# Twelve weight loads per layer of a two-block transformer kernel, each split into a transfer of 120 and one of 8 partitions

## The reference

```python
def peer_ffn(x, w_q, sub_keys, u_tab, v_tab):
    ...
        q = (xc @ w_q).reshape(c, PEER_HEADS, 2, PEER_HALF)
        sc = jnp.einsum('chpd,hpnd->chpn', q, sub_keys).astype(jnp.float32)
        top_s, top_i = lax.top_k(sc, PEER_TOPK)
        ...
        gate = jax.nn.softmax(best_s, axis=-1).astype(xc.dtype)
        u = u_tab[idx]
        act = jax.nn.gelu(jnp.einsum('chkd,cd->chk', u, xc), approximate=False)
        vsel = v_tab[idx]
        return jnp.einsum('chk,chkd->cd', gate * act, vsel)
```

## Time and profile before

| | us |
|---|---|
| time, median of 3 runs | 2322.83 |
| lowest and highest run | 2317.26, 2323.83 |
| profiled execution, its span | 2321.1 |
| DVE busy | 1526.8 (66%) |
| PE busy | 1973.8 (85%) |
| DMA queue of the rows (q0), share of 16 engines | 55.9% |
| DMA queue of SP's loads (q1), share of 16 engines | 20.5% |

### The profile page before, as it was taken

One profiled execution on the slowest core, in us unless ns is written; L12 is line 12 of the kernel. 1 busy time (PEld: TensorE's weight loads), 2 busy tenths in 40 slices (PEclk: granted clock), 3 DMA queues, 4 the chain that ended last, 5 costly groups with the idle time before them and its releaser, 6 DMA issues.

```text
span 2321.1 us, 26066 instructions
## 1 busy us (share of the span) xinstructions
PE 1973.8 (85%) x8576; PEld 1298.3 (56%) x8576; DVE 1526.8 (66%) x3664; ACT 671.8 (29%) x1257; POOL 1232.9 (53%) x824
## 2 busy tenths in 40 slices
PE   7999999999999889887778777798799877777776
PEld 6889998789988764443223222387644433323222
DVE  6441115531117878887888877677798878888776
ACT  6644336644436522111011100156221110111000
POOL 6748867658873256555444444132465554444441
PEclk9999999999999889999999999998899999999999
DMA  5435544435555279999999999662799999999996
GB/s 178 146 112 196 182 162 158 156 117 191 182 178 191 100 296 420 421 420 421 421 421 421 421 420 422 258 221 85 274 410 421 421 421 421 421 422 421 421 421 278
DMA packets 118012, 700.21 MB, mean 302 GB/s; under 512 B 13968, under 2 KB 13968, under 8 KB 51856
## 3 DMA queue, kind: packets, MB, share of 16 engines
q0 software_dynamic: 73728, 536.90, 55.9%
q1 hardware_dynamic: 44176, 161.96, 20.5%
HBM read 697.76 MB, written 1.05 MB: 301 GB/s over the span
## 4 chain that ended last, share of the span: by engine, by line
PE 39%; DMA 39%; DVE 14%; POOL 3%; issue 3%; ACT 2%; DVEq 0%; SPq 0%; POOLq 0%; ACTq 0%
PE ps L637 38%; DMA late_row<-in_table,arena 21%; DMA arena<-in_table,arena 17%; DVE arena L2345 2%; POOL w_split L1222 2%; DVE diag L2355 1%; DVE late_row L2345 1%; DVE arena L2035 1%; DMA row_sb<-in_table,arena 1%; DVE w_split L2021 1%; DVE arena L2319 0%; ACT w_split L1348 0%; POOL arena L1308 0%; PE ps L669 0%; ACT hT_hi L1371 0%
## 5 line engine op out<-in xcount | busy, mean ns | idle before, releaser
L1222 POOL TENSOR_TENSOR w_split<-raw,w_split 128x1024 fp32r<-128x1024 f32 x256 | 623.4, 2459 | 340.4 <-ACT w_split L1348 337.5
L637 PE MATMUL ps<-late_row,diag 128*128 128x512 f32 x1000 | 480.1, 624 | 124.6 <-DVE diag L2355 124.6
L637 PE MATMUL ps<-hT_hi,w_split 128*128 128x256 f32 (+1 forms) x2688 | 521.5, 292 | 15.3 <-POOL w_split L1222 9.6
L637 PE MATMUL ps<-arena,diag 128*128 128x512 f32 x888 | 425.7, 622 | 124.2 <-DVE diag L2355 121.5
L637 PEld LDWEIGHTS ps<-hT_hi,w_split 128*128 128x128 f32 x2688 | 435.5, 196 | 26.4 <-issue 8.3
L1308 POOL DMA_INDIRECT late_row<-in_table,arena x250 | 286.2, 1145 | 305.2 <-PE ps L637 286.9
L637 PEld LDWEIGHTS ps<-late_row,diag 128*128 128x128 f32 x1000 | 188.0, 197 | 406.7 <-DVE diag L2355 212.4
L1308 POOL DMA_INDIRECT arena<-in_table,arena x222 | 250.5, 1129 | 307.2 <-PE ps L637 260.5
L637 PE MATMUL ps<-hT_lo,w_split 128*128 128x256 f32 (+2 forms) x1344 | 386.7, 288 | 0.0
L1678 ACT ACTIVATE arena<-arena 128x2 f32<-128x2 f32 x260 | 52.9, 203 | 1117.3 <-DVE arena L2345 1114.2
L2345 DVE CUSTOM_DVE_ANT_0 late_row<-late_row,x_res 128x1024 f32<-128x1024 f32 x250 | 307.2, 1234 | 104.2 <-DMA late_row<-in_table,arena 104.0
(11 more groups left out here) (266 smaller groups left out, 1839.0 us busy)
## 6 DMA issues: line engine op xcount, KB each, us to landing
raw<-in_stream SPq DMA_DIRECT2D x288, 512.0 KB
row_sb<-in_row SPq DMA_DIRECT2D x2, 2306.5 KB, 11.1
late_row<-in_table,arena POOLq DMA_INDIRECT x250, 30.5
arena<-in_table,arena POOLq DMA_INDIRECT x222, 30.8
arena<-in_sub SPq DMA_DIRECT2D x2, 1024.0 KB, 10.7
arena<-in_small SPq DMA_DIRECT2D x2, 640.0 KB, 8.7
x_res<-in_x SPq DMA_DIRECT2D x1, 1024.0 KB, 5.7
out_x<-x_res SPq DMA_DIRECT2D x2, 512.0 KB, 5.3
```

The lines of the kernel that those rows point to most:

```text
L637: ins = nc.tensor.matmul(o, lhsT, rhs, start=start, stop=stop)
L1222: pool.tensor_tensor(w_lo[pair], raw[:, at % raws, :], w_hi[pair].bitcast(F32), ALU.subtract).then_inc(lo_ready, 1)
```

## The change

In layers of the second block, chunks 30 to 41 (heads 2 to 7) are each loaded by two transfers instead of one: partitions 0 to 119, then partitions 120 to 127. Each adds 16 to the buffer's semaphore. ACT's threshold for a chunk therefore grows by 16 for each split chunk up to this one in the same buffer. The bytes, the buffers and all arithmetic stay.

```diff
+IN_PARTS = range(N2_NARROW, N2)
+FIRST_PART = 120
...
                     if c >= RAW2:
                         low_part_made(sp, c - RAW2)
-                    load(base + c, c % RAW2)
+                    if c in IN_PARTS:
+                        for some in (slice(0, FIRST_PART), slice(FIRST_PART, P)):
+                            sp.dma_start(raw[some, c % RAW2, :], stream[base + c, some]).then_inc(w_ready[c % RAW2], 16)
+                    else:
+                        load(base + c, c % RAW2)
...
-                    act.wait_ge(w_ready[slot], i * (16 * step // self.raws) + 16 * (c // self.raws + 1))
+                    parts = len([k for k in IN_PARTS if k <= c and k % self.raws == slot]) if self.narrow == N2_NARROW else 0
+                    act.wait_ge(w_ready[slot], i * (16 * step // self.raws) + 16 * (c // self.raws + 1 + parts))
```

## The result

The changed kernel takes 2348.7 us (median of 4 runs, 2347.6 to 2351.8), the kernel before 2323.1 us (2317.3 to 2323.8). The ratio is 1.0129, with a 95% interval of 1.0114 to 1.0143: 26 us slower. The forecast was 13 us faster, in a range that ended at 2327 us.

The account below looks back on a forecast made before the run. It took the DMA queues as the bound, one late ring setting each row stretch's end. Gains of 7.0 and 6.0 us, together 13.0, took the 2321.1 us span to 2308.1, median 2310 us; range 2304 to 2327 us with rivals.

Parts of the forecast that it names:

- tails of one ring: At the end of each row stretch one ring works alone at DMA share 0.06, for 7.7 and 7.6 us.
- the relief: Row stretches: the ring without rows of the 120 partitions saves 1.31 us per load, 5.2 to 10.5 us in all.
- The sum, if the spared ring is the late one.: Row stretches' ends: the ring left out by 120 partitions is the late one; 7.0 and 6.0 us gained, together 13.0.
- the first rival: Row stretches: the late ring is not the one left out; 2322.8 to 2325.4 us; chance 0.27, counting no effect with it.
- A transfer of 120 partitions, dealt in eights, is 15 rings with 8 rows each and one ring with none.: Split chunk loads: one ring is relieved of 1.31 us per load; the 8 partitions left add 0.16 us on eight rings.
- The third rival: Split chunk loads: the 120 partitions go over fewer rings; over eight, 2328 or 2344 us; chance 0.09.
- a tail of 7 to 9 us: Sign after the change: one ring alone this long at a row stretch's end means the late ring was not spared.
- the late ring: In row stretches, one ring, not slower but three rows behind the others, sets the end; 7.7 us of lag.
- the packets of q8: Within a row stretch, 11 packets of 1.1 us, 12 us if all on one ring; guessed cause of its lag.

Follow-up runs that it names:

- the probes: Kernel before plus 30 or 40 extra small transfers of few partitions in each row stretch; 2320.3, 2337.4 and 2330.1 us, one execution each.
- the probe with 120: Kernel before plus extra loads of 120 partitions into free buffers beside the rows, one window among other partition counts; 296 GB/s there, whole run 2499.8 us.

## Why the prediction was wrong

The bound, the rates, the stretches and the tails of one ring were read rightly, and that DVE and PE had slack; it is also true that all the effect lies in the loads beside the rows. (Of the second stretch's eight loads five start between 1654 and 1690, not half of them; that bears on the relief alone.) Two steps failed: of the 39 us between the forecast and the measured time the first makes 13 us and the second 26 us.

**"The sum, if the spared ring is the late one."** It is not: by the probes it is one of the second to fourth. The forecast had 0.55 for this, by a judgement on the end of a row of rings that no row bore out. With that step put right (the first rival) the time would have been 2323 to 2325 us, still 23 us too low.

**"A transfer of 120 partitions, dealt in eights, is 15 rings with 8 rows each and one ring with none."** The 15 rings are right (the count of small packets), but the time per row, 0.16 us, and nothing for anyone else, was carried over from the 128 partitions, which cost the rows nothing beyond their bytes. The prediction had said that the deal of 120 was not in the trace; it bounded it by how many rows a ring gets, and never asked where a ring writes. The missing term is 1.63 us per transfer beside the rows, by the probe with 120, so some 26 us for sixteen. The third rival's 2328 to 2344 us came near by its arithmetic, a doubling of a ring's rows, and would have been luck: the rings are not fewer, and the packets are longer.

The prediction said that a tail of 7 to 9 us would mean the first rival; it is 8 us, and that part of it holds. The tail can't see a loss that all rings share. The GB/s at a full share could, and I had named no such reading.

The Trainium skill describes the groups ("DMA: Bandwidth & Descriptors", "The descriptor swizzle"): in a transfer of 128 partitions engine 0 writes partitions 0 to 3 and 32 to 35, and so on, each engine one port; "SBUF — State Buffer" ("Door 1: The DMA port swizzle") gives the ports. These sections give no price for another deal; that comes from the runs here. The probes agree with the groups: partitions 0, 4, ..., 28 cost nothing extra on eight rings (420 GB/s), 64 to 92, on eight rings as well, did (394 GB/s). The prediction named the page's rule on the number of engines, which the packet counts bear out (15 and 8), and passed over this one. The page's remark that engines 7 and 15 are usually the slow ones doesn't help here: the late ring is not slower (25 GB/s alone, where the mean of all is 26.3), and by the rule of the lowest-numbered engines it would be neither of the two.

Open: that the late ring carries the packets of q8 was argued, not shown. Which rings bear the delay of a foreign row is not seen. Which partitions each of the 15 rings writes for a transfer of 120 was not seen either; that they are foreign ones is inferred from the rates. No version here beat the kernel before.

## What to carry to other kernels

When the DMA engines are the bound, count not only how many rows each ring gets but in which partitions it writes: beside saturated transfers, a transfer of all 128 partitions cost only its bytes here, and every other range of partitions tried cost 1.9 to 2.6 times the time of its bytes. Read GB/s beside the DMA share: a full share at fewer GB/s was the sign here that rings hold each other up, and no engine's wait told it apart from a queue that is merely full. Before work is moved off the slowest ring, find out by a small probe which ring that is.

## What the runs showed of the hardware

- 24 more transfers (48 in place of 24 per run), by columns, cost nothing: 1.0001 (0.9991 to 1.0011).
- Beside saturated rows, 417 GB/s with transfers of 128 partitions fell to 292 to 352 GB/s with 32 to 120, at a DMA share of 1.02.
- Eight rows per transfer into partitions 64 to 92 slowed the table rows' packets (336 ns against 314 ns) and hardly their own (164 ns against 161 ns). Transfers of 120 partitions slowed both (0.281 to 0.404 us and 0.146 to 0.200 us, small packets included).
- SP's transfers have one small packet per ring: 16 for 128, 15 for 120 and 8 for 8 partitions, by the totals of q1 (44176 before, 44344 after).
- One ring is alone for the last 7 to 8 us of each row stretch before and after the change; the probes place it second to fourth among the rings that small transfers take, if these always begin with the same ring.
